# A decoder layer's opening: eight adaLN strips of one feature slice each, sums ahead, and one tile squared on VectorE

## The reference, cut to what matters

```
mod = silu(c) @ w_ada + b_ada                 # w_ada is 1024 x 6144
sh_m, sc_m, ... = split(mod, 6)               # shift = cols 0:1024, scale = cols 1024:2048
h = rmsnorm(x, norm_pre_mix) * (1.0 + sc_m) + sh_m
proj = h @ w_in                               # its last 584 columns are the indexer: iq, ik, iw
```

## Time and profile before

| what | value |
| --- | --- |
| time, median of 3 runs | 728.35 us (728.13 to 729.88) |
| the profiled execution: its time, its span | 730.2 us, 728.5 us |
| PE busy of the span | 706.1 us, 97% |
| DVE busy, ACT busy | 439.4 us, 297.3 us |
| mean granted clock of TensorE | 0.989 |
| first indexer product starts | 20.66 us |
| last slice's first product, and the end of its work | 57.22 us, 60.85 us |

### The profile page before, as it was taken

How to read it: one execution, slowest core, us unless ns; L and a number is a source line. 1 busy time by engine, 2 the same in 40 slices (tenths; PEclk the granted TensorE clock), 3 DMA queues, 4 the chain that set the end, 5 groups by cost and what they waited for, 6 DMA issues and landing times.

```text
span 728.5 us, 11027 instructions
## 1 busy us (share of the span) xinstructions
PE 706.1 (97%) x3962; PEld 552.8 (76%) x3962; DVE 439.4 (60%) x814; ACT 297.3 (41%) x478; POOL 10.9 (1%) x39
## 2 busy tenths in 40 slices
PE   5899999999989999999999999999999999999997
PEld 3665567777766878878888888888888788888885
DVE  3966688999898998978653433333432335443444
ACT  6435453635444444535572433432343322211223
POOL 4000000000000000000000000000000000000000
PEclk9899999999999999999899999999999999999999
DMA  9953022241222676567225433455523224323202
GB/s 306 358 149 99 18 58 70 61 132 34 81 60 87 195 224 213 180 210 220 87 58 145 134 95 87 116 144 144 144 88 114 86 87 126 105 87 102 72 0 117
DMA packets 95995, 89.10 MB, mean 122 GB/s; under 512 B 2950, under 2 KB 84954, under 8 KB 95964
## 3 DMA queue, kind: packets, MB, share of 16 engines
q1 hardware_dynamic: 95964, 88.70, 40.4%
HBM read 86.59 MB, written 2.10 MB: 122 GB/s over the span
## 4 chain that ended last, share of the span: by engine, by line
PE 86%; DVE 9%; issue 2%; DMA 2%; ACT 1%; SPq 1%; DVEq 0%
PE ps L1346 49%; PE ps L1367 16%; PE ps L1385 6%; DVE w_lo L818 2%; DMA act<-in_w_ada 2%; PE ps L1567 1%; PE ps L1460 1%; PE ps L1592 1%; PE ps L1648 1%; PE ps L1668 1%; PE ps L1631 1%; PE ps L1406 1%; PE ps L1468 1%; PE ps L1533 1%; PE ps L1780 1%
## 5 line engine op out<-in xcount | busy, mean ns | idle before, releaser
L1346 PE MATMUL ps<-h_hi,w_hi 128*128 128x512 f32 x560 | 227.5, 406 | 0.0
L1346 PE MATMUL ps<-h_hi,w_lo 128*128 128x512 f32 x560 | 218.9, 391 | 0.0
L1346 PE MATMUL ps<-h_lo,w_hi 128*128 128x512 f32 x560 | 218.5, 390 | 0.0
L818 DVE TENSOR_TENSOR w_lo<-w_raw,w_hi 128x1024 fp32r<-128x1024 f32 (+1 forms) x109 | 129.2, 1187 | 99.1 <-ACT w_hi L462 98.8
L462 ACT ACTIVATE w_hi<-w_raw 128x1024 fp32r<-128x1024 f32 (+1 forms) x109 | 111.6, 1029 | 105.1 <-PE ps L1367 86.3
L1346 PEld LDWEIGHTS ps<-h_hi,w_hi 128*128 128x128 f32 x560 | 105.2, 188 | 30.4 <-issue 9.1
L1346 PEld LDWEIGHTS ps<-h_hi,w_lo 128*128 128x128 f32 x560 | 105.1, 188 | 22.5
L1346 PEld LDWEIGHTS ps<-h_lo,w_hi 128*128 128x128 f32 x560 | 105.4, 188 | 20.6 <-issue 1.0
L1367 PE MATMUL ps<-w_hi,h_hi 128*128 128x512 f32 x176 | 70.1, 398 | 0.8 <-DVE mix L1218 0.8
L1367 PE MATMUL ps<-w_hi,h_lo 128*128 128x512 f32 x176 | 68.6, 390 | 0.0
L1367 PE MATMUL ps<-w_lo,h_hi 128*128 128x512 f32 x176 | 68.6, 390 | 0.0
(11 more groups left out here) (254 smaller groups left out, 799.7 us busy)
## 6 DMA issues: line engine op xcount, KB each, us to landing
w_raw<-in_w_ffn_in SPq DMA_DIRECT2D x44, 512.0 KB, 5.6
w_raw<-in_w_in SPq DMA_DIRECT2D x28, 512.0 KB, 4.0
w_raw<-in_w_ffn_out SPq DMA_DIRECT2D x22, 512.0 KB, 3.5
adaw<-in_w_ada SPq DMA_DIRECT2D x12, 512.0 KB, 4.0
act<-in_w_ada SPq DMA_DIRECT2D x12, 512.0 KB, 9.3
adaw<-in_w_ada SPq DMA_DIRECT2D x6, 1024.0 KB, 5.3
act<-in_w_ada SPq DMA_DIRECT2D x6, 1024.0 KB, 5.3
res<-in_x SPq DMA_DIRECT2D x8, 512.0 KB, 5.0
```

What stands on the lines that cost most here:

```text
L818: V.tensor_tensor(w_lo[slot][:, 0:n], w_raw[slot][:, 0:n], w_hi[slot][:, 0:n].bitcast(f32), ALU.subtract).then_inc(lo_ok, 1)
L1346: last = mm(ps[bank][0:rows, :], a, b, start=(k == 0 and n == 0), stop=(k == KT - 1 and n == 2))
```

## The change

Constants and loads: `ADA_COLS` is 256, and a strip set now belongs to one slice: all eight contraction tiles, 128 shift and 128 scale columns (512-byte runs). Eight `copy_rows`, eight `start_sums` and eight `start_mods` replace four of each; each handles half as many columns. The parameters are issued ahead of the first w_ada load, each w_ada slice is issued next to its indexer weights, and the two norm parameters of the indexer go behind the first four slices with a semaphore of their own, for which VectorE waits where it uses them. TensorE computes slice 1's strips ahead of slice 0's products, later slices' strips two slices ahead, and the sums one slice ahead, after the first four products of a slice. The angles are cut in thirds over six slices. VectorE squares and sums the last tile of x.

```diff
 def load_start_ada(n):
-    pair, half = n // 2, n % 2
-    slot = start_slot[n].rearrange("p (k n) -> p k n", k=4)
+    slot = start_slot[n].rearrange("p (k n) -> p k n", k=KT)
     for a, col in enumerate((0, D_MODEL)):
-        sp.dma_start(slot[:, :, a * 2 * P:(a + 1) * 2 * P],
-                     w_ada[0]...[:, 4 * half:4 * half + 4, col + pair * 2 * P:col + (pair + 1) * 2 * P])
+        sp.dma_start(slot[:, :, a * P:(a + 1) * P],
+                     w_ada[0]...[:, :, col + n * P:col + (n + 1) * P])
# SP, order of the issues
-            load_start_ada(0)
-            load_start_ada(1)
             ... # b_ada, norms, lower bound
+            load_start_ada(0)
             load_idx(0)
+            load_start_ada(1)
+            load_idx(1)
             ... # positions, rope_const
-            ... # the two norm parameters
-            load_idx(1)
             load_start_ada(2)
+            load_idx(2)
             load_start_ada(3)
-            load_idx(2)
             load_idx(3)
+            ... # the two norm parameters, on knorm_loaded
             sp.wait_ge(xt_mm, 2 * TT)
+            for n in range(4, KT):
+                if n >= 6:
+                    sp.wait_ge(ada_used, n - 5)
                 load_start_ada(n)
+                sp.wait_ge(lo_ok, n - 3)
+                load_idx(n)
# ACT, row_stats
+                if not seen and t == TT - 1:
+                    sc.wait_ge(xsq_ok, 1)
+                    sc.sem_inc(ss_ok, 1)
+                else:
                     sc.activation(... ACT.Square, accum_out=ss[:, t:t + 1]).then_inc(ss_ok, 1)
# ACT, order
             row_stats(0, 2)
+            row_stats(0, 3)
             copy_xt_low(0)
-            row_stats(0, 3)
-            for pair in range(4):
-                if pair:
-                    split_idx(2 * pair)
-                copy_rows(pair)
-                if pair == 0:
-                    split_idx(0)
-                split_h(2 * pair)
-                split_idx(2 * pair + 1)
-                split_h(2 * pair + 1)
-                if pair in (1, 2):
-                    sines(2 - pair)
+            copy_rows(0)
+            split_idx(0)
+            for k in range(KT):
+                if k < KT - 1:
+                    if k == 0:
+                        copy_rows(1)
+                    split_h(k)
+                    if k:
+                        copy_rows(k + 1)
+                    split_idx(k + 1)
+                else:
+                    split_h(k)
+                if k in (3, 6):
+                    sines(1 if k == 3 else 0)
# VectorE
             norm_rows(0, 1)
-            copy_xt_high(0)
+            ve.wait_ge(x_loaded[TT - 1], 16)
+            V.tensor_tensor_reduce(out=junk_last, in0=xr[:, 3072:4096], in1=xr[:, 3072:4096], scale=1.0, scalar=0.0,
+                                   op0=ALU.mult, op1=ALU.add, accum_out=ss[:, TT - 1:TT]).then_inc(xsq_ok, 1)
             norm_rows(0, 2)
-            copy_xt_high(1)
             norm_rows(0, 3)
-            copy_xt_high(2)
-            copy_xt_high(3)
+            for t in range(TT):
+                copy_xt_high(t)
...
-            for pair in range(4):
-                start_mods(pair)
-                feature_in(2 * pair)
-                feature_in(2 * pair + 1)
-                feature_lo(2 * pair)
-                split_lo(2 * pair + 1, (2 * pair + 1) % 4, IDX_COLS)
-                feature_lo(2 * pair + 1)
-                ... # all angles of a kind in pairs 0 and 1
-                if pair < 3:
-                    split_lo(2 * pair + 2, (2 * pair + 2) % 4, IDX_COLS)
+            for k in range(KT):
+                start_mods(k)
+                feature_in(k)
+                if k < KT - 1:
+                    split_lo(k + 1, (k + 1) % 4, IDX_COLS)
+                feature_lo(k)
+                if k == 0:
+                    ve.wait_ge(pos_loaded, 32)
+                    astep(V.tensor_copy(pos, pos_i[:, :].bitcast(i32)))
+                if k < 6:
+                    angles(1 - k // 3, k % 3)
# TensorE
-            start_ada(0)
             ... # transpose of the parameters
+            start_ada(0)
             te.wait_ge(prm_ok, 1)
             start_sums(0)
-            idx_high(0, IDX_ORDER)
-            idx_low(0)
-            for pair in range(1, 4):
-                start_ada(pair)
-                idx_high(2 * pair - 1, IDX_ORDER[:2])
-                start_sums(pair)
-                idx_high(2 * pair - 1, IDX_ORDER[2:])
-                idx_low(2 * pair - 1)
-                idx_high(2 * pair, IDX_ORDER)
-                idx_low(2 * pair)
-            idx_high(KT - 1, IDX_ORDER)
-            idx_low(KT - 1)
+            start_ada(1)
+            for k in range(KT):
+                idx_high(k, IDX_ORDER[:2])
+                if k == 1:
+                    start_ada(2)
+                    idx_high(k, IDX_ORDER[2:4])
+                    start_sums(2)
+                    idx_high(k, IDX_ORDER[4:])
+                else:
+                    if k < KT - 1:
+                        start_sums(k + 1)
+                    idx_high(k, IDX_ORDER[2:])
+                idx_low(k)
+                if 1 <= k < KT - 2:
+                    start_ada(k + 2)
```

More of the change, by code:

```diff
@@ L858, in norm_rows, with angles @@
                                 rstd[:, t:t + 1], None, ALU.mult).then_inc(xn_ok, 1)
-            def angles(kind, second_half):
+            def angles(kind, third):
                 a, turns = ang[2 * kind + 1], ang[2 * kind]
-                if not second_half:
+                if third == 0:
                     astep(V.tensor_scalar(a, pos, rc[:, 2 * kind:2 * kind + 1], None, ALU.mult))
@@ L949, in _, with start_mods @@
             ve.wait_ge(xt_high, TT)
[L951 to L956 removed]
+            def start_mods(k):
+                ve.wait_ge(start_cols, k + 1)
+                V.tensor_tensor(mod[:, 0:16].rearrange("p (a j) -> p a j", a=2)[:, :, k],
+                                ps[6][:, 0:2], prm[:, 0:16].rearrange("p (a j) -> p a j", a=2)[:, :, k],
                                 ALU.add).then_inc(start_mod, 1)
[L958 to L960 removed]
+                ve.wait_ge(start_mod, k + 1)
+                V.scalar_tensor_tensor(out=scale_mix[:, k:k + 1], in0=mod[:, 8 + k:9 + k], scalar=1.0,
+                                       in1=prm[:, C_PRE_MIX + k:C_PRE_MIX + k + 1], op0=ALU.add,
                                        op1=ALU.mult).then_inc(start_scale, 1)
[L962 removed]
+                ve.wait_ge(start_scale, k + 1)
             def feature_in(k):
@@ L1409, in ada_mm @@
             def ada_mm(bank, strip, k, w, first, last_one):
-                return mm(ps[bank][strip * 32:(strip + 1) * 32, :], silu_pad[:, k * 32:(k + 1) * 32], w, start=first,
-                          stop=last_one)
-            def ada_half(bank, half, w):
-                for strip in range(4):
-                    last = ada_mm(bank, strip, 4 * half + strip, w[:, strip * ADA_COLS:(strip + 1) * ADA_COLS],
-                                  half == 0, half == 1)
-                last.then_inc(ada_used, 1)
+                return mm(ps[bank][strip * 32:(strip + 1) * 32, 0:ADA_COLS], silu_pad[:, k * 32:(k + 1) * 32], w,
+                          start=first, stop=last_one)
             te.wait_ge(c_loaded, 16)
@@ L1434, in _, with start_ada, start_sums @@
             te.wait_ge(silu_ok, 1)
-            def start_ada(pair):
-                if pair:
-                    te.wait_ge(start_rows, pair)
-                for half in range(2):
-                    te.wait_ge(start_loaded[2 * pair + half], 32)
-                    ada_half(7, half, start_slot[2 * pair + half])
-            def start_sums(pair):
-                te.wait_ge(start_rows, pair + 1)
-                if pair:
-                    te.wait_ge(start_mod, pair)
-                for q in range(4):
+            def start_ada(n):
+                if n:
+                    te.wait_ge(start_rows, n)
+                te.wait_ge(start_loaded[n], 32)
+                for k in range(KT):
+                    last = ada_mm(7, k % 4, k, start_slot[n][:, k * ADA_COLS:(k + 1) * ADA_COLS], k < 4, k >= 4)
+                last.then_inc(ada_used, 1)
+            def start_sums(n):
+                te.wait_ge(start_rows, n + 1)
+                if n:
+                    te.wait_ge(start_mod, n)
+                for q in range(2):
                     last = mm(ps[6][:, q:q + 1], ada_rows[:, q * P:(q + 1) * P], ones[:, 0:1], start=True, stop=True)
```

79 lines of the change are left out of this document (28 added, 51 removed).

## The result

The changed kernel takes 738.64 us in the median of four executions (738.0 to 741.29), the kernel before 728.58 on the same chip: a ratio of 1.0146 [1.0128, 1.0164]: slower. The forecast was 735.0 (730.5 to 741.0) with 0.81 on slower. A second set of four executions of the same kernel, taken later, has a median of 735.51 (734.78 to 739.66) and a ratio of 1.0106 [1.0080, 1.0132]. What can part the two sets is shown under E8.

The account below looks back on a forecast made before the run. In the opening, VectorE's round, waits included, was to decide: last slice +6.4 us, ScalarE's end +0.2, sum +6.6, so 728.35 + 6.6 = 735.0 us. Range 730.5 to 741 (8 in 10).

Parts of the forecast that it names:

- The round, the step that decides: VectorE's round in the opening: 3.78 us plus its third of the angles, 1.5 of it idle; last slice +6.4 us.
- The first two slices: PE's slice 0 from 19.9 us at half clock, slice 1 at 26.3, then mods 2 at 32.7.
- The front: Loads up to slice 0: slice 1's strips land at 17.8 us, PE starts slice 0 at 19.9, 0.8 earlier.
- covered by 2 us: VectorE's reduction of x's last tile is over before slice 1's strips land at 17.8 us: cost and gain 0.
- The end: Close of the opening: slice 7 starts at 63.6 us against 57.22, +6.4; with ScalarE's end +0.2, sum +6.6.
- ScalarE's end: ScalarE's table load and two full splits behind `split_h(7)` end at 66.9 us, PE's bank ready at 66.5: +0.2.
- PE's work a slice: PE in the opening: 3.46 + 0.93 for strips + 0.4 for sums = 4.8 us, as before per slice.
- The last tile of x: Square and sum on VectorE instead of ScalarE: takes 1.2 us, cost and gain 0.
- PE stays the bound: Rival, chance 0.11: VectorE's wait is short, only the front and PE's work count, opening 58.5 against 60.7, 726.2 us.
- It cancels: Rival, chance 0.07: half the idle time hidden and the front 1.1 us earlier leave +1.0, 729.4 us.
- The clock falls: Rival, chance 0.12: gaps each round halve PE's clock, five slices add 5 to 10 us, 740 to 745.
- the likeliest case: The main forecast, chance 0.70, with its own range of 732.5 to 738 us.

Follow-up runs that it names:

- E8: The changed kernel measured again, with no edit: 735.51 us, ratio 1.0106.
- E1: Changed kernel with ScalarE splitting slice k+1's weights ahead of `split_h(k)` and copying the rows behind it: 730.4 us, ratio 1.0025.
- E6: Changed kernel with only `copy_rows(k+1)` moved behind `split_idx(k+1)`, both still behind `split_h(k)`: 733.98 us, ratio 1.0063.
- E3: Changed kernel with the last tile of x squared on ScalarE again, PSUM copies in the order of before: 738.12 us, ratio 1.0132.
- E5: Changed kernel with w_ada loaded in 1 KB runs, same bytes and order, shift and scale not the slice's: 736.45 us, ratio 1.0114.
- E4: E1 with `split_h(0)` ahead of `copy_rows(1)` and slice 1's strips and sums inside slice 0: 729.8 us, ratio 1.002.
- E9: E4 with the later memset of E2 and four idle products of 256 columns ahead of slice 0: 728.62 us, ratio 0.9994.
- E2: Changed kernel with GpSimd's memsets moved behind the last indexer product: 737.95 us, ratio 1.0128.
- E7: Changed kernel with the angles whole again, after slices 0 and 2, instead of in thirds: 745.35 us, ratio 1.023.

## Why the prediction was right

**The round, the step that decides: right.** The mods of slices 2 to 7 came at 33.30, 40.16, 45.84, 51.78, 58.65 and 62.42 us. The rounds are 6.86, 5.68, 5.94, 6.87 and 3.77 us; forecast were 6.88, 5.69, 5.96, 6.88 and 3.78. The idle time is 1.55 us (forecast 1.5), and E1 and E6 show that ScalarE's order makes it: take the piece out and PE is the bound, shorten it by 0.27 and every round shortens by 0.27. The durations of the earlier trace rows carried over to the new order because both engines alternate in it; nothing else reached into the round. PE's slice followed the mods by 1.75 us (33.30 to 35.05) instead of 1.63.

**The first two slices: close, but by another path.** The forecast had slice 0 at half clock and slice 1 at 26.3, set by PE. In the first profile slice 0 ran at the full clock and was done at 24.9, and slice 1 started at 26.65, 1.75 us behind VectorE's mods 1 (24.90). That it is only 0.35 us off is luck: the late front and the faster slice 0 offset each other. In E8 the forecast's path held, with slice 0 at half clock from 20.25, slice 1 at 26.92 without a wait, and mods 2 at 33.52 (33.30 in the first profile, forecast 32.7).

**The front: 0.9 us short.** The loads behaved as said (slice 1's strips wait for theirs in E3 and E8, and start at 17.91 and 18.07, forecast 17.8), at 302 to 316 GB/s with full queues rather than 292 and against 350 before. The Trainium skill (DMA: Bandwidth & Descriptors, Specifications) gives 512 bytes as the smallest transfer at line rate. The runs here differ: E5 gives 353 to 366 GB/s with 1 KB runs and the same bytes. But slice 0 started at 20.79 in the first profile, not 19.9; it was 20.25 in E8. In the first profile the transposes of x's tiles 2 and 3 ran slowly:

```profile
12.04 3.68 PE L1419 MATMUL ps<-ident,act 128*128 128x128 f32 x16 [0.94 <-DVE act L858]
```

The same 16 took 2.03 us in E1, E4 and E9, 2.11 in E2, 2.88 in E7 and 3.68 again in E6. It is the clock, though the views show 1.00 there. The trace has no clock record before 16.74 us in this execution, and a view counts what stands before the first record as 1.00. The groups by form tell it by the mean length of one transpose (number after the comma): the kernel before from 356 to 359.8 us, at a clock of 0.50; then these 16; then those of E9, whose first record, 1.00, stands at 10.17 us.

```profile
L1406 PE MATMUL ps<-ident,act 128*128 128x128 f32 x20 | 4.5, 423 | 0.0
```
```profile
L1419 PE MATMUL ps<-ident,act 128*128 128x128 f32 x16 | 3.7, 424 | 0.9 <-DVE act L858 0.9
```
```profile
L1418 PE MATMUL ps<-ident,act 128*128 128x128 f32 x16 | 2.0, 280 | 1.6 <-DVE act L857 1.6
```

In all twelve profiles the transposes ahead of the first record are long and those behind it short; it stands at 16.74 and 16.77 us in the first profile and E6, at 10.2 to 13.5 in the others. So slice 1's strips, at 18.40, did not wait for their load there, and what I had called covered by 2 us was not. This term was read as a sum of VectorE's work alone; a PE at the lower clock in the front was not in it.

**The end: 0.55 us not seen.** `feature_in(7)` took 1.10 instead of 0.55 us beside the memsets (E2). After the change the last sines release them just ahead of the last `feature_in`; I had not asked what their new place releases. ScalarE's end was +0.15, forecast +0.2. Mods 2 to 7 all came 0.5 to 0.6 us after their forecast (what the front had left over), and with 0.55 for the memsets slice 7 started at 64.72 instead of 63.6: +7.5 for the forecast +6.4, and +7.65 for +6.6 at the end of the opening.

**PE's work a slice: 5.05, not 4.8 us.** The strips cost 1.00 in a row (taken 0.93), the sums 0.36 plus a longer first product behind them. It doesn't matter where VectorE sets the round; it counts in E1, where it takes back what the closed gap gives: from slice 0 to slice 7 PE needs 36.46 us, against 36.56 before with a gap of 1.09 in it. That E1's opening ends 0.8 us later than before comes from its later slice 0 (21.41 against 20.66).

**The last tile of x: right.** The reduction took 1.23 us (taken 1.2), and E3 gives the same ratio without it.

```profile
10.00 1.23 DVE L936 CUSTOM_DVE_ANT_0 rope<-res 128x1024 f32<-128x1024 f32 x1 [1.12 <-DMA res<-in_x]
```

**The rivals.** "PE stays the bound" was wrong for this kernel, since ScalarE's splits did not come out ahead; E1 is that rival's case by construction, and it gave 730.4, not the 726.2 that I had put there. Its opening ended at 61.58 instead of the rival's 58.5, though the half clock in slice 0 was in that sum: slice 0 started 1.5 us later (slice 1's strips waited for their load and took 1.92 us at the lower clock), slices 1 to 6 took 30.59 instead of 28.74 us, the last 3.71 instead of 3.46, and slice 0 5.87 instead of 6.4. "It cancels" is ruled out by the rounds. "The clock falls" was half right. In the first profile the gaps of up to 1.76 us left the clock at 1.00. With the same rounds, or rounds 0.27 us shorter, it fell in slice 0 in E2, E3, E5, E6 and E8, and once more in a single later slice in E2, E3 and E5, not in five; these openings end 0.2 to 1.6 us after the first profile's (E2, E3, E5, E8), not 5 to 10.

**The time.** The median of 738.64 lies 3.6 over the forecast: inside the range of 730.5 to 741, outside the 732.5 to 738 given for the likeliest case. The opening explains 1.1 of it. The second set's 735.51 lies 0.5 over the forecast. All eight executions of this kernel spread from 734.8 to 741.3, with 738.05 in the middle; the clock at 360 us is good for up to 3.2 of that spread. How much of the rest it is can't be told, since only one execution of a set is profiled. The time outside the span was 1.9 us against 1.7; why is open.

## What to carry to other kernels

When two engines hand work to each other, write down for each item which engine is idle until the other is done. An independent piece of work (here the weight split for the next slice) belongs ahead of the instruction that waits, not behind it: the same work in the other order was worth 6.9 us of the opening. Price a finer pipeline by its round with the waits in it, from the durations of before, and read an edit's effect at the end of the stage that it touches, before the total.

## What the runs showed of the hardware that was not expected

- TensorE's clock fell to half while PE had no gap. In the kernel before PE is busy 2.00 of every 2 us from 340 to 354, the fall comes between 352 and 354, in a row of 32 sums of one column that starts at 351.04, and holds through them and into the transposes of 128 columns (0.50 from 355 to 360 us). It comes in some executions of one kernel and not in others (E8), for up to 3.2 us. What decides it is open.
- A view's granted clock is 1.00 up to the trace's first clock record, whatever the clock was: the 16 transposes of the front took 3.68 us in two profiles and 2.03 in three, under the same 1.00. The length of one transpose (424 or 280 ns) tells the two apart.
- Slice 0 ran at 1.00 behind four idle products of 256 columns (E9), where the clock fell to 0.50 in E1, E4 and E8. But it ran at 1.00 without them in the first profile and in E7, so one profile doesn't show that they did it.
- With full queues w_ada in 512-byte runs, beside the indexer's weights, moved at 302 to 316 GB/s, in 1 KB runs at 353 to 366.
- A VectorE instruction of 0.55 us that meets two memsets in a row on GpSimd, which read nothing, ends 0.27 to 0.29 us after the second, at 1.10 to 1.41 us in all: it isn't let in between them.
